# Storing a matmul's moving operand by halves of its columns, 256 bytes out of step

## The reference

```python
# first block, layer l
h = hybrid_mixer(x, w_in[l], ...)                  # x @ w_in: 1024 x 7680, attention, branches, @ w_mix_out
x = layer_norm(alpha * x + h, ln_g[l, 0], ln_b[l, 0])
h = memory_cross_attention(x, mem, xa_q[l], ...)   # x @ xa_q, mem @ xa_kv, attention, @ xa_o
x = layer_norm(alpha * x + h, ln_g[l, 1], ln_b[l, 1])
h = conv_ffn(x, ffn_w_in[l], ...)                  # x @ ffn_w_in: 1024 x 5632, conv, silu, @ ffn_w_out
x = layer_norm(alpha * x + h, ln_g[l, 2], ln_b[l, 2])
# second block, layer l
x = x + 0.5 * swiglu(rms_norm_2(x, ffn1_norm[l]), ffn1_gate[l], ffn1_up[l], ffn1_down[l])   # 1024 x 2816, twice
h = rms_norm_2(x, mix_norm[l]) @ w_in[l]           # pooling, two attentions, convolution, @ w_out
x = x + 0.5 * swiglu(rms_norm_2(x, ffn2_norm[l]), ffn2_gate[l], ffn2_up[l], ffn2_down[l])
```

## Time and profile before

| | |
|---|---|
| runs | 2125.45, 2125.82, 2138.95 us (median 2125.82) |
| profiled execution | 2125.48 us, of which the span from first to last instruction is 2123.7 us |
| mean granted TensorE clock | 0.993 of full speed |
| PE busy | 2081.9 us (98% of the span), 17304 matmuls |
| DVE busy | 1436.2 us (68%) |
| ACT busy | 994.2 us (47%) |
| weights read | 336 chunks of 1 MB, mean 172 GB/s |

### The profile page before, as it was taken

How to read it: one execution, slowest core, us unless ns; L and a number is a source line. 1 busy time by engine, 2 the same in 40 slices (tenths; PEclk the granted TensorE clock), 3 DMA queues, 4 the chain that set the end, 5 groups by cost and what they waited for, 6 DMA issues and landing times.

```text
span 2123.7 us, 39278 instructions
## 1 busy us (share of the span) xinstructions
PE 2081.9 (98%) x17304; PEld 2030.7 (96%) x17304; DVE 1436.2 (68%) x1690; ACT 994.2 (47%) x1166; POOL 78.8 (4%) x96
## 2 busy tenths in 40 slices
PE   7999999999999999998999999999999999999998
PEld 7999999999999999998999999989999999989997
DVE  6665574676776655747667775797666666897564
ACT  4554454444455544544444444455444444454442
POOL 1000010100010000101000100000000000000000
PEclk9999999999999999999999999999999999999999
DMA  5444554455544445534555355534555555434552
GB/s 211 154 164 161 193 187 150 152 192 198 199 163 154 164 162 195 184 130 161 192 180 178 142 199 194 183 120 144 196 198 193 185 194 189 176 117 159 199 191 87
DMA packets 52858, 365.94 MB, mean 172 GB/s; under 512 B 5904, under 2 KB 5904, under 8 KB 9296
## 3 DMA queue, kind: packets, MB, share of 16 engines
q1 hardware_dynamic: 52272, 361.21, 47.5%
q0 software_dynamic: 416, 2.22, 0.3%
HBM read 362.35 MB, written 1.05 MB: 171 GB/s over the span
## 4 chain that ended last, share of the span: by engine, by line
PE 87%; issue 9%; DVE 2%; POOL 1%; ACT 0%; DMA 0%; POOLq 0%; DVEq 0%; ACTq 0%
PE accM L1156 51%; PE scoreP L1156 18%; PE outP L1156 9%; PE turnP L1156 8%; PE turnP L1342 1%; DVE wlo L1599 1%; POOL x L727 1%; POOL small L713 0%; PE outP L1368 0%; PE turnP L1395 0%; ACT whi L782 0%; DMA x<-in_xT 0%; DVE xl L1739 0%; DVE diag L1774 0%; DVE small L1776 0%
## 5 line engine op out<-in xcount | busy, mean ns | idle before, releaser
L1599 DVE TENSOR_TENSOR wlo<-raw,whi 128x2048 fp32r<-128x2048 f32 x336 | 768.3, 2289 | 349.3 <-ACT whi L782 348.4
L782 ACT ACTIVATE whi<-raw 128x2048 fp32r<-128x2048 f32 x336 | 639.9, 1910 | 233.6 <-PE accM L1156 135.9
L1156 PE MATMUL accM<-xh,whi 128*128 128x256 f32 x1152 | 336.6, 292 | 5.5 <-DVE xl L1739 4.8
L1156 PE MATMUL scoreP<-xh,whi 128*128 128x256 f32 x1152 | 323.0, 280 | 7.9 <-DVE xl L1622 4.3
L1156 PE MATMUL accM<-xh,wlo 128*128 128x256 f32 x1152 | 322.9, 280 | 0.0
L1156 PE MATMUL accM<-xl,whi 128*128 128x256 f32 x1152 | 322.9, 280 | 0.0
L1156 PE MATMUL scoreP<-xl,whi 128*128 128x256 f32 x1152 | 321.1, 279 | 0.0
L1156 PE MATMUL scoreP<-xh,wlo 128*128 128x256 f32 x1152 | 321.0, 279 | 0.0
L1156 PE MATMUL accM<-fh,wlo 128*128 128x256 f32 x1056 | 292.5, 277 | 0.0
L1156 PE MATMUL accM<-fl,whi 128*128 128x256 f32 x1056 | 292.5, 277 | 0.0
L1156 PE MATMUL accM<-fh,whi 128*128 128x256 f32 x1056 | 292.5, 277 | 0.0
(11 more groups left out here) (283 smaller groups left out, 4164.1 us busy)
## 6 DMA issues: line engine op xcount, KB each, us to landing
raw<-in_W SPq DMA_DIRECT2D x336, 1024.0 KB, 4.8
biasr<-in_bias SPq DMA_DIRECT2D x16, 256.0 KB, 3.0
raw<-in_memT SPq DMA_DIRECT2D x2, 1024.0 KB, 4.9
cc<-in_consts POOLq DMA_DIRECT2D x1, 1408.0 KB, 6.8
x<-in_xT SPq DMA_DIRECT2D x4, 256.0 KB, 4.5
out<-x SPq DMA_DIRECT2D x4, 256.0 KB, 2.9
c<-in_consts SPq DMA_DIRECT2D x1, 464.5 KB, 6.3
par<-in_par POOLq DMA_DIRECT2D x2, 203.5 KB, 3.7
```

Source lines behind the costliest of these rows:

```text
L782: nc.scalar.activation(whi[:, hi_slot(c), :], raw[:, raw_slot(c), :], ACT.Copy).then_inc(split_hi.sem, 1)
L1156: return nc.tensor.matmul(dst, a, b, start=start, stop=stop, skip_group_check=True)
L1599: v.tensor_tensor(wlo[:, raw_slot(c), :], raw[:, raw_slot(c), :], whi[:, hi_slot(c), :].bitcast(F32), ALU.subtract).then_inc(split_lo.sem, 1)
```

## The change

`xh` and `xl` become views of one tensor `xhl` of `[128, 2, 2112]`. Its second axis t is the half of the tokens: tokens 0 to 127 of all eight k, first of `xh`, then of `xl`, and then the same for tokens 128 to 255, 2112 numbers (8448 bytes, which is 256 modulo 512) further on. `_lead` shrinks from 48 to 16 numbers, so that in the built program the first half of every k starts at 192 modulo 512 bytes and the second at 448. `_trail` shrinks as well, so that no other tensor moves. A row tile k of `xh` is then two runs of 512 bytes in place of one of 1024.

An F product streams both runs in one matmul: its moving operand has the pattern 2 x 128 in place of 256. A T product holds one run of 128 tokens, which now starts at 192 for m = 0 and at 448 for m = 1. ACT and DVE write and read the two runs in one instruction, through `by_halves`. No other operand is stored differently.

```diff
--- before.py
+++ after.py
@@ -254,10 +254,13 @@
         wlo = sb("wlo", [P, RAW_RING, CH], F32R)
         whi = sb("whi", [P, HI_RING, CH], F32R)
         x = sb("x", [P, KT, S])
-        _lead = sb("lead", [P, 48])
-        xh = sb("xh", [P, KT, S], F32R)
-        xl = sb("xl", [P, KT, S], F32R)
-        _trail = sb("trail", [P, 80])
+        _lead = sb("lead", [P, 16])
+        halves = ExitStack()
+        xhl = sb("xhl", [P, 2, 2 * KT * P + 64], F32R, halves)
+        halves.close()
+        _held = sb("held", [P, 4 * KT * P + 64])
+        _trail = sb("trail", [P, 48])
+        xh, xl = (xhl[:, :, i * KT * P:(i + 1) * KT * P].rearrange("p t (k s) -> p k t s", k=KT) for i in range(2))
         c0 = sb("c0", [P, NC0])
         ones = sb("ones", [P, P])
         par = sb("par", [P, NP1])
@@ -456,6 +459,10 @@
             if n == END1 + 1:
                 return c0[:, C0["first_g"][0] + k:C0["first_g"][0] + k + 1]
             return col("norm_g", ((n - END1 - 1) % 3) * KT + k, 1, P2)
+
+        def by_halves(rows):
+
+            return rows.rearrange("p (t s) -> p t s", t=2)
 
         def affine(n, k):
 
@@ -797,7 +804,7 @@
             def upper(n, b):
 
                 for k in (2 * b, 2 * b + 1):
-                    ins = nc.scalar.activation(xh[:, k, :], x[:, k, :], ACT.Copy, scale=gain(n, k))
+                    ins = nc.scalar.activation(xh[:, k, :, :], by_halves(x[:, k, :]), ACT.Copy, scale=gain(n, k))
                 ins.then_inc(xhi.sem, 1)
 
             def square(n, b):
@@ -849,7 +856,7 @@
                         else:
                             act.wait_ge(centred.sem, centred.at((n, b)))
                         g, bb = affine(n, k)
-                        ins = nc.scalar.activation(xh[:, k, :], cen[:, b % 2, m * S:(m + 1) * S], ACT.Identity,
+                        ins = nc.scalar.activation(xh[:, k, :, :], by_halves(cen[:, b % 2, m * S:(m + 1) * S]), ACT.Identity,
                                                    bias=bb, scale=g)
                     ins.then_inc(xhi.sem, 1)
                 if between and n <= END1 and n not in covered:
@@ -1202,6 +1209,14 @@
                     a_hi, a_lo = fh[:, c["j"] % 2, :, :], fl[:, c["j"] % 2, :, :]
                 if r in ("xk", "xv"):
                     await_split(pe, c["mem"])
+                split = a_hi is xh
+
+                def streamed(a, k):
+                    return a[:, k, :, :] if split else a[:, k, :]
+
+                def held(a, k, m):
+                    return a[:, k, m, :] if split else a[:, k, m * P:(m + 1) * P]
+
                 if kind in ("F", "T"):
                     for name in claims[c["c"]] if k0 == 0 else []:
                         bank[name].claim(pe, *taker(c))
@@ -1216,12 +1231,13 @@
                             first, last = k == 0 and m == 0, k == KT - 1
                             o = dst[:, m * S:(m + 1) * S]
                             if kind == "F":
+                                o = by_halves(o) if split else o
                                 w_hi, w_lo = hi[:, k, m * P:(m + 1) * P], lo[:, k, m * P:(m + 1) * P]
-                                mm(o, w_hi, a_hi[:, k, :], first, False)
-                                mm(o, w_hi, a_lo[:, k, :], False, False)
-                                ins = mm(o, w_lo, a_hi[:, k, :], False, last)
+                                mm(o, w_hi, streamed(a_hi, k), first, False)
+                                mm(o, w_hi, streamed(a_lo, k), False, False)
+                                ins = mm(o, w_lo, streamed(a_hi, k), False, last)
                             else:
-                                t_hi, t_lo = a_hi[:, k, m * P:(m + 1) * P], a_lo[:, k, m * P:(m + 1) * P]
+                                t_hi, t_lo = held(a_hi, k, m), held(a_lo, k, m)
                                 mm(o, t_hi, hi[:, k, :], first, False)
                                 mm(o, t_hi, lo[:, k, :], False, False)
                                 ins = mm(o, t_lo, hi[:, k, :], False, last)
@@ -1619,7 +1635,7 @@
 
                 dve.wait_ge(xhi.sem, xhi.at((n, b)))
                 for k in (2 * b, 2 * b + 1):
-                    ins = v.scalar_tensor_tensor(xl[:, k, :], x[:, k, :], gain(n, k), xh[:, k, :].bitcast(F32),
+                    ins = v.scalar_tensor_tensor(xl[:, k, :, :], by_halves(x[:, k, :]), gain(n, k), xh[:, k, :, :].bitcast(F32),
                                                  ALU.mult, ALU.subtract)
                 ins.then_inc(xlo2.sem, 1)
 
@@ -1736,7 +1752,8 @@
                     dve.wait_ge(xhi.sem, xhi.at((n, b)))
                     dve.wait_ge(xnew.sem, xnew.at((n, b)))
                     k = slice(2 * b, 2 * b + 2)
-                    v.tensor_tensor(xl[:, k, :], x[:, k, :], xh[:, k, :].bitcast(F32), ALU.subtract)\
+                    v.tensor_tensor(xl[:, k, :, :], x[:, k, :].rearrange("p k (t s) -> p k t s", t=2),
+                                    xh[:, k, :, :].bitcast(F32), ALU.subtract)\
                         .then_inc((xlo1 if b else xlo0).sem, 1)
 
                 if n == LAST:
```

## The result

| | before | after |
|---|---|---|
| median of 5 runs each | 2132.62 us | 2154.14 us |
| lowest, highest | 2125.45, 2140.71 | 2151.90, 2157.43 |
| profiled execution | 2125.48 us, span 2123.7 | 2157.43 us, span 2155.6 |

The ratio is 1.0095, with an interval from 1.0066 to 1.0123. The change makes the kernel some 21 us slower by the medians, where 28 us less was predicted. The runs after lie within 6 us of each other, those before within some 15.

The account below looks back on a forecast made before the run. It took PE's matmul count times their distance as the bound: 18.3 us and 10.0 us saved on x's F products, 28 us off 2125.5, gave 2097.5, predicted as 2098 us. The 8-in-10 range was 2074 to 2158 us.

Parts of the forecast that it names:

- 28 us less: F products of x: 18.3 us from 3100 on the upper level, 10.0 us from 6690 on the lower.
- the distance between matmuls is the bound: Whole kernel: PE busy 98% of the span, so time is the number of matmuls times their distance, plus little else.
- the writers' cost: ACT and DVE writing two runs of 512 bytes in place of one: taken as nothing; under 1 us with 5%.
- the surplus comes from the moving read meeting the load of the weights: Matmuls of x: less collision after the change, given 0.44, from 2074 to 2111 us.
- no effect: Rival: the two reads don't meet, products of x keep their mix of levels; 2112 to 2136 us, chance 0.34.
- the load fills the whole stream: Each matmul: the load of 128 columns, 512 bytes, fills nearly the whole distance between matmuls.
- 111.7 ns, the distance of the loads in the earlier trace: Price taken for F products of x after the change, from seven loads starting (0.86 - 0.19) / 6 apart.
- The 109.4 ns of the far end: Lowest price considered for F products of x: 22.5 us more gain, so 51 us.
- every product on the lower level: Weak outcome for F products of x: all at 113.2 ns, 3100 x 4.4 = 14 us gained.
- the slower one: Rival: the change makes the kernel slower, 2140 to 2170 us; chance 0.22.
- 6690 x 4.8: Slower rival's term for x: 6690 is the F products of x estimated on the lower level before.
- The T products: 672 products of x whose held run starts at 192 or 448 in place of 320: 3 us either way, taken 0.

Follow-up runs that it names:

- dist_176: Kernel before with x's parts, still in a single run, moved 16 bytes earlier: distance 176 from the weights' start in place of 192; ratio 1.0187.
- two_from_320: Changed kernel with `_lead` at 48, so its two runs start at 320 and 64 modulo 512; 2135.96 us, ratio 1.0011 to before.
- two_in_step: Changed kernel's two runs of 128 columns, but 2048 numbers apart, both starting at 320 modulo 512; 2133.97 us, ratio 1.0005 to before.
- kick_xh: Kernel before with the last row tile (k = 7) of `xh` 64 bytes later, putting 816 F products at distance 0; 2118.39 us, ratio 0.9959.
- dist_256: Kernel before with x's parts in one run starting at 384 modulo 512, 256 bytes after the weights, thus distance 0; 2168.80 us, ratio 1.0175.

## Why the prediction was wrong

**That the distance between matmuls is the bound: right.** All of the 32 us is PE's. With it the writers' cost (nothing), the unchanged order and waits, and the two levels of 113.3 and 117.8 ns at full clock held.

**That the surplus comes from the moving read meeting the load of the weights: made likely, not shown.** The surplus is what a matmul takes over 106.7 ns. No run shows this figure at full clock; as an estimate it is half of the 213.3 ns that six matmuls of x took each while the granted clock was 0.50, and 113.3 and 117.8 ns lie 6.6 and 11.1 ns above it. That these are a meeting of two reads, that of the moving operand and that of the next weights, was my assumption. What is shown is that the spacing depends on where the two operands start relative to each other: moving the weights in place of x's parts changes the spacing of `fh`, `yh`, `mh`, `oh`, `zh` and x alike, and the T products, in which the parts are exchanged, follow the distance in the main. Where I gave 0.34 to "no effect", the argument was that a collision set by addresses should give one level in both FFNs. It overlooked that one distance can have two levels. At equal work and equal clock, the addresses alone move the kernel by up to 1.87% (`dist_176`).

**That the load fills the whole stream: open.** The place of both halves counts, as it would then, but a cost of the jump between them isn't excluded.

**The step that failed** is the one from the layout to a price: that two runs 256 bytes out of step meet the load for less of the time than one run does, and so lose most of the surplus. That step gave the change its gain. It rested on an assumption of mine on how the two reads are served, and no row and no run shows it. The runs show three things against it. The jump of 256 bytes halfway through the stream does nothing (`two_from_320` at 1.0011 against `two_in_step` at 1.0005). I took the start of a single run to be without effect, yet it moves the matmul from 113.3 to 119.8 ns. And 192 and 64, which I thus held to be alike for one run, have the same two levels but not the same share of them: at 192, which the change gave up, two thirds of x's F products were on the lower level, at 64 some 3%. The change thus cost 26 us on x's F products, where I had predicted 28 us of gain. I had marked the assumption as one that no row shows, and still let it choose the sign.

**That 111.7 ns, the distance of the loads in the earlier trace rows, is the price after:** never reached. No distance in any kernel gave a chain row of x products below 10.88 us for 96, which is 113.3 ns each. That a load of this size is a floor for the next matmul isn't shown either: the row gives the distance of seven loads ahead of 64-column matmuls, and no more. The 109.4 ns of the far end is shown by no run, and nothing came near it. So even the sign given right, the gain left would have been the 14 us of "every product on the lower level". `kick_xh` is 8 us faster than the kernel before, but only some 3 us of that are x's.

**The rival that happened** is the slower one, given 0.22: from the new start, 64 bytes after the weights' in place of 192, every F product of x is on the upper level, 6690 x 4.8 = 32 us more, 2158 us. The profiled execution was 2157.43. That the two agree so closely is luck: 2158 counts x alone, and with the further 12 us that I gave it for `fh` and the like the rival would stand at 2170. Its terms: 32 us for x, measured 26, since the mean before was 114.92 and more products were on the upper level already than the windows let me count; 12 us for `fh` and the like if they follow, measured 7, since they follow in some stretches only. Its reason, that the new start meets the load for longer, isn't shown by any run.

**The T products** were bounded at 3 us either way and taken at 0. They gained 1.5 us, with the distance (192) that the F products lost.

**The range** of 2074 to 2158 us holds the median of 2154.14, near its upper end.

What stays open: why 192 and 64 bytes, and for 192 within less than 16 of them, have prices that the other distances don't reach; why two levels exist there, and why long stretches of x take the lower one at 192 and the upper one at 64, while `yh` and `mh` did the reverse; and why, after x at 64, `fh` comes down in some FFNs and not in others. The runs give the relation, not the mechanism, and no record in the trace shows single reads.

## What to carry to other kernels

Where matmuls with a weight load each follow one another without a gap, count matmuls per window first: two levels in the same code at the same clock (here 113.3 and 117.8 ns at 1.00) say that something other than work and clock sets the pace, and here the operands' addresses moved it from 113.3 to 119.8 ns. Then treat the distance of the two operands' starts modulo 256 bytes as a setting of its own and measure a few values, from weights or operand, before any argument on how the memory serves the reads is trusted; in the pattern of the operand (one run, or two in step) there was nothing to gain or to lose here (1.0005). A kernel whose runs fall into groups at equal steps (here near 2119, 2126 and 2133 us) may have such a state, and here displacing one row tile of eight put all twelve runs within 2 us of each other, at the better end.

## What was unexpected of the hardware

- Fp32r matmuls of 256 columns, each with a load of 128, follow each other in 113.3 ns at best, and up to 119.8 ns with the distance between operands, at a granted clock of 1.00.
- 176 and 208 bytes give 119.3 and 119.2 ns, 192 between them gives 113.3 or 117.8. 64 has the same two levels, and which one is taken isn't fixed by the distance: `yh` and `mh` were at 117.8 with 192 and at 113.3 with 64, long stretches of x in the FFNs mostly the reverse.
- At a distance of 192 a stream kept its level for the 1400 matmuls of a window (1414 in 160 us at 430 us, 1483 in 175 us at 985 us). With 816 products at distance 0 between them, all four FFNs profiled were on the lower one, though each 96 products took 10.95 us for 10.88 and a product at 0 costs 119.8 ns in `dist_256`.
- A moving operand in two runs of 128 columns costs nothing: 1.0005 [0.9983, 1.0027] with both in place.
